# Two-layer diffusion step with grouped experts on one Trainium2 core: the last expert tile added on chip, and a down product moved into a gate/up product

## The reference

```python
act = silu(einsum('td,edf->tef', t, w_gate)) * einsum('td,edf->tef', t, w_up)
act = act * gates[..., None]            # zero for experts that were not picked
moe = einsum('tef,efd->td', act, w_down)
x = x + g_f * moe                       # g_f: one row for latent, one for context tokens
h = modulate(rmsnorm(x, norm_mix[l + 1]), shift, scale)   # layer 0: input of layer 1
y = rmsnorm(x, norm_final)                                 # layer 1: the output
```

## Time and profile before

| | us |
|---|---|
| median of three runs | 1364.23 |
| lowest and highest of them | 1360.12, 1364.32 |
| the profiled execution, its own time | 1358.21 |
| its span, first to last instruction | 1356.2 |
| PE busy, DVE busy, ACT busy, POOL busy | 1232.8, 581.4, 331.4, 235.4 |
| mean granted TensorE clock | 0.981 |

### The profile page before, as it was taken

One profiled execution on the slowest core, in us unless ns is written; L12 is line 12 of the kernel. 1 busy time (PEld: TensorE's weight loads), 2 busy tenths in 40 slices (PEclk: granted clock), 3 DMA queues, 4 the chain that ended last, 5 costly groups with the idle time before them and its releaser, 6 DMA issues.

```text
span 1356.2 us, 19957 instructions
## 1 busy us (share of the span) xinstructions
PE 1232.8 (91%) x7783; PEld 712.6 (53%) x7783; DVE 581.4 (43%) x1494; ACT 331.4 (24%) x783; POOL 235.4 (17%) x298
## 2 busy tenths in 40 slices
PE   4999899999999999998949999998889998999991
PEld 3665466666645644444424455555775455444440
DVE  5221355555535764443431000003774566444443
ACT  4121344444412300000122000003773330000012
POOL 7121400100100011232220100104221001221231
PEclk9999999999999999999979999999999999999996
DMA  9413211321574389999680443244214435999966
GB/s 385 169 40 135 113 64 64 113 77 64 225 266 156 137 295 385 385 387 371 170 267 33 181 177 125 72 175 166 72 49 180 199 121 228 384 386 376 342 159 205
DMA packets 45452, 267.87 MB, mean 198 GB/s; under 512 B 6980, under 2 KB 13460, under 8 KB 31520
## 3 DMA queue, kind: packets, MB, share of 16 engines
q1 hardware_dynamic: 22672, 192.85, 36.4%
q0 software_dynamic: 16928, 52.77, 14.3%
q10 hardware_dynamic: 5760, 20.97, 4.0%
HBM read 230.19 MB, written 34.81 MB: 195 GB/s over the span
## 4 chain that ended last, share of the span: by engine, by line
PE 71%; DMA 15%; DVE 6%; ACT 4%; issue 4%; DVEq 0%; ACTq 0%; POOLq 0%; SPq 0%; POOL 0%
PE PS L893 13%; DMA xrows<-big,info 12%; PE PS L1256 10%; PE PS L1118 10%; PE PS L1166 9%; PE PS L1021 4%; PE PS L1183 4%; PE PS L758 4%; PE PS L1061 3%; PE PS L764 3%; PE PS L780 3%; DMA xrows<-big 3%; PE PS L980 2%; PE PS L1318 1%; DVE big L1663 1%
## 5 line engine op out<-in xcount | busy, mean ns | idle before, releaser
L1118 PE MATMUL PS<-weights,ht 128*128 128x512 f32 x320 | 142.3, 596 | 1.7 <-DVE ht L1663 0.9
L1256 PE MATMUL PS<-ht,weights 128*128 128x128 f32 (+1 forms) x512 | 140.2, 434 | 1.5 <-PE PS L780 0.9
L758 PE MATMUL PS<-const,big 128*128 128x128 f32 (+2 forms) x611 | 89.6, 283 | 36.6 <-DVE big L2196 17.5
L893 PE MATMUL PS<-weights,ht 128*128 128x336 f32 (+1 forms) x320 | 117.8, 526 | 2.6 <-ACT ht L1442 1.7
L758 PEld LDWEIGHTS PS<-const,big 128*128 128x128 f32 (+2 forms) x611 | 74.0, 144 | 82.6 <-issue 56.8
L1166 PE MATMUL PS<-big 128*128 128x512 f32 x256 | 113.0, 594 | 3.4 <-DVE big L2113 3.4
L1256 PEld LDWEIGHTS PS<-ht,weights 128*128 128x128 f32 x512 | 77.8, 191 | 64.1 <-issue 64.1
L1118 PEld LDWEIGHTS PS<-weights,ht 128*128 128x128 f32 x320 | 59.0, 190 | 69.1 <-issue 69.1
L1572 ACT ACTIVATE big<-PS 128x256 f32<-128x256 f32 x34 | 13.0, 383 | 325.4 <-PE PS L1166 325.4
L893 PEld LDWEIGHTS PS<-weights,ht 128*128 128x128 f32 x320 | 60.8, 193 | 54.2 <-issue 40.7
L698 POOL DMA_INDIRECT xrows<-big,info x28 | 47.8, 1707 | 221.1 <-DMA xrows<-big,info 213.5
(11 more groups left out here) (250 smaller groups left out, 1759.6 us busy)
## 6 DMA issues: line engine op xcount, KB each, us to landing
weights<-in_ada SPq DMA_DIRECT2D x22, 2048.0 KB, 8.4
big<-in_gu SPq DMA_DIRECT2D x16, 2048.0 KB, 17.0
weights<-in_gu SPq DMA_DIRECT2D x12, 2048.0 KB, 21.8
rows<-in_down SPq DMA_DIRECT2D x18, 1024.0 KB, 12.8
weights<-in_down SPq DMA_DIRECT2D x16, 1024.0 KB, 17.4
ht<-in_gu SPq DMA_DIRECT2D x6, 2048.0 KB, 22.1
weights<-in_qkv SPq DMA_DIRECT2D x6, 2048.0 KB, 9.8
weights<-in_wo SPq DMA_DIRECT2D x4, 2048.0 KB, 7.9
```

Source lines behind the costliest of these rows:

```text
L758: return pe.transpose(dst, src, const[0:n, C_ID:C_ID + n])
L893: ins = pe.matmul(bank(4 + u % 2, n), lhs(k), rhs(k), start=(k == 0), stop=(k == ks - 1))
L1118: ins = pe.matmul(bank(4 + j), OT[:, k, t * P:(t + 1) * P], w[j][:, k, :], start=(k == 0), stop=(k == KD - 1))
L1256: ins = pe.matmul(bank(bb, n1 - n0), w[:, k, m * P:(m + 1) * P], hT[:, k, n0:n1], start=(k == 0), stop=(k == KD - 1))
```

## The change

Two things change, in both layers.

First, the last tile (16) is no longer added in HBM. The reload of the residual waits for the adds of tiles 14 and 15 only. DVE builds a matrix `at_token` of zeros and ones (128 slots by 640 tokens) out of the token numbers of the last tile. PE multiplies the scaled rows of tile 16 by it, one tile of tokens at a time (`last_part`: two products of 512 columns, four instructions, into two PSUM banks), and DVE adds the result to the reloaded tile (`x_sum`, 128x1024). Parts 0 to 3 have their own banks; part 4 uses those of part 3 and waits for its sum. In layer 0 `ada(1, 4)` stands before the parts, and part 4 stands behind the first value product and the transposes of tile 2. ACT and DVE norm a tile after its sum.

Second, in the loop PE forms the down product of tile 15's predecessor as before, but the pass's own first down product (tile 15) is placed inside the gate/up product of tile 16, after two of its eight steps. DVE's program is rearranged with it.

```diff
@@ gpsimd, after the loop
-                pool.wait_ge(e_yd[l], trips * 2 + STAT)
-                pool.wait_ge(e_ys[l][1], trips * 16 + 16 * 7)
-                pool.nop().then_inc(e_gate, 1)
-                add_rows(last_token(2), 0)
@@ tensor
+                        if k == 2 and between is not None:
+                            between()
...
-                    for j in range(2):
-
-                        gateup(j, e_gw[l][j], i * 16 + 16, i * 2 + (STAT + 1 + j))
-                        if j == 0:
-                            rows_T(j, i * 16 + 16 * 8)
-                        down(2 + j, e_dw[l][j], i * 16 + 16, i * 2 + (STAT + j), i * 2 + (STAT - 1 + j))
-                        acts_T(i * 2 + (STAT + 1 + j))
+                    gateup(0, e_gw[l][0], i * 16 + 16, i * 2 + (STAT + 1))
+                    rows_T(0, i * 16 + 16 * 8)
+                    down(2, e_dw[l][0], i * 16 + 16, i * 2 + STAT, i * 2 + (STAT - 1))
+                    acts_T(i * 2 + (STAT + 1))
+                    gateup(1, e_gw[l][1], i * 16 + 16, i * 2 + (STAT + 2),
+                           lambda: down(3, e_dw[l][1], i * 16 + 16, i * 2 + (STAT + 1), i * 2 + STAT))
+                    acts_T(i * 2 + (STAT + 2))
                 down(2, e_dw[l][0], trips * 16 + 16, trips * 2 + STAT, None, 3)
...
+                if l == 0:
+                    ada(1, 4)
+                pe.wait_ge(e_yd[l], trips * 2 + STAT)
+                pe.wait_ge(e_sel, l + 1)
+                for t in range(4):
+                    last_part(l, t)
+
+            def last_part(l, t):
+
+                if l == 0 and t == 3:
+                    pe.wait_ge(m_cp, 17)
+                if t == 4:
+                    pe.wait_ge(c_sum, NT * l + 4)
+                for n in range(2):
+                    ins = pe.matmul(part_at(t)[:, n * 512:(n + 1) * 512], at_token[:, t * P:(t + 1) * P], yb[0][:, n * 512:(n + 1) * 512],
+                                    start=True, stop=True)
+                ins.then_inc(c_part, 1)
...
-            ada(1, 4)
...
+                if u == 0:
+                    pe.wait_ge(c_sum, 3)
                 v_unit(u)
                 if u < 3:
                     x_transposes("m1", u + 2)
+                if u == 0:
+                    last_part(0, 4)
...
             moe(1)
+            last_part(1, 4)
@@ scalar
-                act.wait_ge(e_ys[l][0], trips * 16 + 16 * 8)
-                act.wait_ge(e_ys[l][1], trips * 16 + 16 * 7)
+                for par in range(2):
+                    act.wait_ge(e_ys[l][par], trips * 16 + 16 * 7)
                 if l == 0:
                     act.wait_ge(m_mm, 17)
                 for t in range(NT):
                     act.dma_start(x_(t), xD[l][t * P:(t + 1) * P, :]).then_inc(c_in[t], 16)
+                for par in range(2):
+                    act.wait_ge(e_gi[l][par], trips * 16 + 16 * 8)
@@ vector
-                base = 3 * (STAT - 1)
+                base = 3 * STAT
+                gate_rows(last[:, 0, 0:1], base - 2, base - 1)
                 trips = dve.value_load(rtx[0:1, 31:32], min_val=1, max_val=5)
                 with dve.Fori(0, trips) as i:
                     rows_T(i * 2 + (STAT + 1))
                     dve.wait_ge(e_gr[l], i * 8 + base)
...
+            def x_sum(l, t):
+
+                dve.wait_ge(c_part, NT * l + t + 1)
+                dve.wait_ge(c_in[t], 16 * (l + 1))
+                tt(x_(t), x_(t), part_at(t), ALU.add).then_inc(c_sum, 1)
```

More of the change, by code:

```diff
@@ L239, in build, with part_at @@
         gfin = HT[:, 4096:4096 + D]
+        at_token = big(2304, NT * P)
+        def part_at(t):
+            return PS[:, 2 * (t if t < 4 else 3) * 512:2 * (t if t < 4 else 3) * 512 + D]
         modD = nc.dram_tensor("modrows", [DEPTH, 2, 6 * D], F32).ap()
@@ L323, in build @@
         c_in = [sem(f"x_back{t}") for t in range(NT)]
+        e_sel = sem("last_slots_in_token_order")
+        c_part, c_sum = sem("last_rows_in_token_order"), sem("x_summed")
         (e_tr, e_ta, e_td, e_gu, e_sg, e_ga, e_ac, e_at, e_ae, e_dn, e_gr, e_yd) = (
@@ L1158, in rows_T, with gateup @@
                     ins.then_inc(e_tr[l], 1)
-                def gateup(b, w_in_, w_ready, rows_ready):
+                def gateup(b, w_in_, w_ready, rows_ready, between=None):
                     pe.wait_ge(w_in_, w_ready)
@@ L1413, in norm_fin @@
                     if t < NT:
-                        act.wait_ge(c_in[t], 32)
+                        act.wait_ge(c_sum, NT + t + 1)
                         rms("fin", t)
@@ L1607, in _ @@
                 if t < NT:
-                    act.wait_ge(c_in[t], 16)
+                    act.wait_ge(c_sum, t + 1)
                     rms("m1", t)
@@ L1675, in norm_fin @@
                 rs = st[:, 50 + 5 * i:55 + 5 * i]
+                x_sum(1, 0)
                 for t in range(NT):
+                    if t < NT - 1:
+                        x_sum(1, t + 1)
                     rstd("fin", t)
@@ L2164, in moe @@
                     dve.wait_ge(e_gr[l], i * 8 + base)
[L2165 to L2174, removed]
+                    acts(last[:, 1, 1:2], i * 2 + (STAT + 1), i * 2 + STAT)
+                    rows_T(i * 2 + (STAT + 2))
+                    acts_T(i * 2 + (STAT + 1))
+                    y_out(i * 2 + STAT, i * 8 + base, 0, i * 16 + 16 * 7)
+                    gate_rows(last[:, 0, 1:2], i * 8 + (base + 1), i * 8 + (base + 2))
+                    y_out(i * 2 + (STAT + 1), i * 8 + (base + 3), 1, i * 16 + 16 * 7)
+                    gate_rows(last[:, 0, 2:3], i * 8 + (base + 4), i * 8 + (base + 5))
+                    acts(last[:, 1, 2:3], i * 2 + (STAT + 2), i * 2 + (STAT + 1))
+                    acts_T(i * 2 + (STAT + 2))
                     dve.wait_ge(e_gr[l], i * 8 + (base + 6))
@@ L2179, in moe @@
                 dve.wait_ge(e_gr[l], trips * 8 + base)
-                gate_rows(last[:, 0, 0:1], trips * 8 + (base + 1), trips * 8 + (base + 2))
-                y_out(trips * 2 + STAT, trips * 8 + (base + 3), 0, trips * 16 + 16 * 7, 3)
+                link(dve.tensor_scalar(rs_[:, 122:123], last[:, 0, 0:1].bitcast(U32), 1.0, None, ALU.add))
+                link(tt(rs_[:, 123:128], rs_[:, 122:123].to_broadcast([P, NT]), const[:, C_E128:C_E128 + NT], ALU.subtract))
+                tt(at_token.rearrange("p (t n) -> p t n", t=NT), rk[:, K_IOTA:K_IOTA + P].unsqueeze(1).to_broadcast([P, NT, P]),
+                   rs_[:, 123:128].unsqueeze(2).to_broadcast([P, NT, P]), ALU.is_equal).then_inc(e_sel, 1)
+                y_out(trips * 2 + STAT, trips * 8 + base, 0, trips * 16 + 16 * 7, 3)
+            def x_sum(l, t):
+                dve.wait_ge(c_part, NT * l + t + 1)
+                dve.wait_ge(c_in[t], 16 * (l + 1))
+                tt(x_(t), x_(t), part_at(t), ALU.add).then_inc(c_sum, 1)
             f_stage(0)
             moe(0)
+            ada_rows(16)
+            x_sum(0, 0)
             def v_out(u):
@@ L2191, in _ @@
             for t in range(NT + 1):
+                if t < NT - 1:
+                    x_sum(0, t + 1)
                 if t < NT:
@@ L2208, in _ @@
                     v_out(u)
+                if n >= 2:
                     ada_rows(15 + n)
```

## The result

| | us |
|---|---|
| changed kernel, median of 22 runs (lowest, highest) | 1366.44 (1361.90, 1371.51) |
| kernel before, median of 22 runs beside them | 1363.37 (1358.28, 1367.42) |
| ratio, 95% interval | 1.0032 [1.0019, 1.0044] |
| span of the profiled execution, before and now | 1356.2, 1360.1 |

The time lies in the range, but the forecast was no change, and the changed kernel is slower: by 3.1 us in the medians (3.9 us between the two traces), and clear of noise. Everything that the change meant to remove is gone from the trace. The third add is gone, the reload starts earlier, PE idles less before the value product. What came instead is read at the loop's entry and at the ends of the two layers.

A forecast was written before the change was run, and what follows sets the result against it. POOL's adds were taken to bound each expert stage's end. Layer 0 -1.8, layer 1 -1.3, clock 2 x 1.2 and 0.4 sum to -0.3 us: about 1364 us (no change, 0.66), range 1358.8 to 1368.4.

The forecast's parts named there:

- The clock: Rival: three thin places on PE each cost their full fall to half clock; +4.1 us, 1368.3 us, chance 0.14.
- The third add: POOL's last add at each expert stage's end is removed: 6.3 us in layer 0, 6.1 us in layer 1.
- The loop's entry: Gate operations moved ahead of tile 15's row copy start its gate/up 2.23 us later in both layers; PE idles 3.8 us.
- The clock at the entry: PE's clock falls to half behind the entry gap: 0 to 1.7 us lost, taken 1.2, in each layer.
- Tile 14's add: POOL's add leaves about 2 us later in both layers; in layer 0 it still takes 10.75 us.
- the rival of a quick add: Rival: layer 0's tile 14 add was slow only through its neighbours and lands in 6.2 us; 1357.3 us, chance 0.09.
- The sum on DVE: Adding PE's part to a reloaded tile, 128x1024 with one operand in PSUM, takes 1.28 us; nothing hides it.
- Layer 0's end: Reload starts at 689.2 instead of 694.11, transposes at 696.85 instead of 700.50; layer 0 gains 1.8 us in all.
- Layer 1's end: Reload starts 8 us earlier, but DVE sets the pace and last scaling ends at 1351.0 instead of 1352.32: -1.3 us.
- signs that the prediction itself had listed as wrong: Short entry gap, layer 0's tile 14 add near 6 us, sums of 0.7 us, DVE waiting for parts 0 to 3.
- The entries are 14 us of dense work away from the end: Argument against the slow clock rival: 14 us of dense work lie between the loop's entries and the end.
- The rule against gaps: Skill's rule: an idle PE array falls to half rate; with both entry falls in full the sum would be +0.7 us.

The follow-up runs named there:

- experiment 1: Changed kernel with tile 14's gate rows moved back behind the copy of tile 15's rows: 1356.92 us, 0.9971 of the kernel before.
- experiment 2: Kernel before with tile 14's gate rows built ahead of the copy of tile 15's rows, the next two tiles' placed as in the change: 1372.42 us, ratio 1.0082.
- experiment 10: Kernel before with tile 14's gate rows ahead of the copy, plus four products on constants on PE in the entry gap: 1366.22 us, 1.0028 of the kernel before.
- Experiments 3: Changed kernel with four products on constants keeping PE busy in the gap at the loop's entry: 1361.56 us, 0.9995 of the kernel before.
- Experiment 7: Changed kernel with tile 14's gate rows behind the copy and layer 1's part 4 directly behind the other parts: 1352.96 us, 0.9926 of the kernel before.
- experiment 4: Changed kernel with layer 1's part 4 in part 0's banks, directly behind the other parts: 1364.23 us, 1.0025 of the kernel before.
- experiment 6: Changed kernel with the loop order of before on PE and DVE, so only the last tile is kept on chip: 1358.60 us, 0.9975 of the kernel before.

## Why the prediction was wrong

The likeliest case was no change, at about 1364, and a slower kernel had 0.15. The mechanism was right in most of its steps. The step that failed is the one on the clock, by its size: "0 to 1.7 us lost, taken 1.2" in each layer at the entry, and "0 to 1.7; taken 0.4" for part 4. In the trace of the changed kernel these three places cost 1.5, 3.0 and 1.8 us, 6.3 in place of 2.8. A smaller step failed beside it: the end of layer 0, by DVE's wait for tile 1. What came is close to the rival called *The clock*, at +4.1 us with a chance of 0.14.

- *The third add* (6.3 and 6.1 us). Right: gone in both layers.
- *The loop's entry* (2.23 us later). Right: 2.4 us in layer 0 (4.04 against 1.60 behind the transposes) and 2.6 in layer 1. Experiments 1, 2 and 10 show that it counts, and the trace of experiment 10 that it counts nearly in full.
- *The clock at the entry.* Wrong size. The bound of 1.7 us came from the one fall that the trace of before shows in busy work. In layer 0 it took 1.5 us, within that; in layer 1 the clock stayed at half twice as long (the product took 10.15 us, 3.05 more). Experiments 3 and 10 price it at 5 and 7 us for the two layers, with wide intervals, against my 2.4. With 5 in place of the 2.4 the sum of -0.3 becomes +2.3, measured were +3.1. The trace agrees: 4.5 for the entries (+2.1 on my sum), 1.8 for part 4 (+1.4) and the later transposes of layer 0 (+1.35) turn -0.3 into +4.6, and the two layers come out at +4.7 there.
- *Tile 14's add.* Right: 10.76 us in flight in layer 0 as before, so the rival of a quick add fell; 3.7 us later behind the entry, 3.2 forecast with the clock. In layer 1 it left 5.6 us later behind the entry where 3.4 were forecast, by the longer stretch at half clock.
- *The sum on DVE* (1.28). 1.22.
- *Layer 0's end.* The reload came 3.4 us earlier behind the entry (3.7 forecast with the clock), but the transposes only 1.1 (2.45). My time for them leaves room for tile 1's sum only if tile 1 is back within 1.5 us of tile 0 (ACT's work on tile 0); it came 2.7 behind, and with its sum ahead of tile 0's reciprocal DVE stood 1.50 us. The prediction named DVE's order and not this wait. No experiment changes that order, so its price of 1.05 us is read from one trace.
- *Layer 1's end.* I had the last part and the reload within 0.2 us of each other and named that as the point from which the slow rival decides. Tile 0's sum started 1.4 us behind the estimated return of the reload, for want of part 0, and part 4 ran at half clock (1.8 us lost, 0.4 taken, 1.7 given as the most). DVE's waits for parts 0 and 1 (2.25 and 0.50 us) are one of the signs that the prediction itself had listed as wrong. The reload started 5.5 us earlier behind the entry, where 6.8 were forecast with the clock. Experiment 7 takes part 4's slow run and the wait for sum 3 away, and leaves the wait for part 0.
- *"The entries are 14 us of dense work away from the end"*, which I had against the slow rival, is no argument: in layer 0 what is lost at the entry is lost to tile 14's add, and the adds end the layer; in layer 1 it is lost to PE's own work up to the parts. I had used the first of these for the 2.23 us in the part on the loop's entry.
- *The rule against gaps* was on the right side. The Trainium skill (TensorE: Matmul & The Clock Gate, Why this matters for your kernels) warns against such gaps, and both entries of the changed kernel fell to half. By it the sum was +0.7, still short. That the trace of before agrees was right at 687 us, with PE idle since 683, and loosely read at 465 us: PE's longest idle time in the 3 us before that fall is 0.91 us, and it was busy for 1.65 of the 3 us. The falls behind short waits in layer 0 of the changed kernel (1.45 and 0.52 us) and in experiment 7 (1.94 us) came without a long gap too.

What stays open: why the same gap costs 1.5 us once and 3.0 another time, and what of the down product's move is its own. The layer doesn't decide the first: in experiment 2 the longer one is in layer 0, in the changed kernel in layer 1, and in the trace of experiment 4, whose program is the changed kernel's up to layer 1's parts, the products take 10.16 us in layer 0 and 8.61 in layer 1.

## What to carry to other kernels

When a block of work is moved on an engine with idle time, ask who waits for the instruction that it now stands ahead of; two and a half microseconds in front of one copy, in each of two layers, cost 8 us here (experiment 1), more than the 3 us that the removal of a six-microsecond add from each layer gained (experiment 6). Price a new idle gap of TensorE twice, as a wait and as half clock behind it, and if the gap can't go, a few products that nobody reads can be worth their place. When an accumulation buffer is reused at the tail, give the last piece the buffer that comes free first, not the one that comes free last.

## What the runs showed of the hardware

- In the kernel of experiment 7, a gap of 1.94 us at layer 0's entry was also followed by a slow product (8.80 us), while gaps of 1.31 us at an entry were not in any trace of this case, nor one of 1.59 us. Idle time alone doesn't sort them: behind waits of 1.45 and 0.52 us at tile 16's sigmoid the last down product took 5.40 us in layer 0 of the changed kernel and 3.70 in layer 1.

```profile
652.87 8.80 PE L1172 MATMUL PS<-big 128*128 128x512 f32 x16 [1.94 <-DVE big L2145]
```

- Tile 14's add, an accumulating indirect DMA of 128 rows, took 10.8 us in layer 0, where 3 MB of weights are loaded beside it, and 6.3 us before and 6.0 us after the change in layer 1, where 1 MB is. No run takes the loads away, so that they are the cause isn't shown.
- Of the five transfers of the reload, 512 KB each and issued one behind the other from one queue, the second landed 2.7 us behind the first in layer 0 of the changed kernel.
